# Two halves of the activations through one high weight matrix in the down projections

## The reference

```python
# first_block, twice: w_down is 4096 x 1024
hn = rmsnorm(h, gains[2])
ff = jnp.square(jax.nn.relu(hn @ w_up[layer])) @ w_down[layer]
h = h + rmsnorm(ff, gains[3])
gate = jax.nn.sigmoid(h @ w_ple_gate[layer])
h = h + gate * (p[layer] @ w_ple[layer])
# second_block, twice: ffn_w_down is 2816 x 1024
gate = _causal_dwconv(xn @ ffn_w_gate[l], ffn_conv_w[l], ffn_conv_b[l])
x = x + (jax.nn.silu(gate) * (xn @ ffn_w_up[l])) @ ffn_w_down[l]
```

## Time and profile before

| | |
|---|---|
| three runs | 1644.57, 1646.49, 1647.23 us |
| the profiled execution | 1639.38 us |
| its span, first to last instruction | 1637.9 us |
| TensorE matmuls: busy, count | 1492.3 us, 10862 |
| VectorE: busy, count | 1024.2 us, 1491 |
| ScalarE: busy, count | 778.5 us, 1205 |
| mean granted TensorE clock | 0.955 |
| DMA | 228.44 MB, mean 139 GB/s |

### The profile page before, as it was taken

One profiled execution on the slowest core, in us unless ns is written; L12 is line 12 of the kernel. 1 busy time (PEld: TensorE's weight loads), 2 busy tenths in 40 slices (PEclk: granted clock), 3 DMA queues, 4 the chain that ended last, 5 costly groups with the idle time before them and its releaser, 6 DMA issues.

```text
span 1637.9 us, 26038 instructions
## 1 busy us (share of the span) xinstructions
PE 1492.3 (91%) x10862; PEld 1406.7 (86%) x10862; DVE 1024.2 (63%) x1491; ACT 778.5 (48%) x1205; POOL 158.1 (10%) x136
## 2 busy tenths in 40 slices
PE   6877987999998877999999998899999988999999
PEld 5865877999987667999998787799999777899999
DVE  4653447765467855665467675577866666587763
ACT  5322424544446453444336666444445666554443
POOL 0002232110000001211010000011000000011100
PEclk9988998999999999999999997999999998899999
DMA  7431203555545314465544421355556431246563
GB/s 240 129 103 52 99 5 106 177 182 180 182 154 179 128 53 129 135 194 185 186 154 155 143 87 52 97 172 168 188 180 198 142 113 52 78 145 189 167 199 101
DMA packets 186388, 228.44 MB, mean 139 GB/s; under 512 B 5920, under 2 KB 161056, under 8 KB 186272
## 3 DMA queue, kind: packets, MB, share of 16 engines
q1 hardware_dynamic: 185264, 222.01, 42.2%
q0 software_dynamic: 1008, 4.77, 0.8%
HBM read 225.72 MB, written 1.05 MB: 138 GB/s over the span
## 4 chain that ended last, share of the span: by engine, by line
PE 65%; DVE 20%; ACT 9%; issue 4%; POOL 0%; DMA 0%; ACTq 0%; DVEq 0%; SPq 0%; POOLq 0%
PE bank L492 19%; PE bank L493 18%; PE bank L494 18%; DVE weights_low L767 7%; ACT weights_high L665 5%; PE bank L500 2%; PE bank L1894 2%; PE bank L974 2%; DVE cv L2732 2%; ACT S L1944 2%; PE bank L1873 1%; DVE cv L2729 1%; DVE S L2018 1%; DVE pad L2719 1%; DVE h L868 1%
## 5 line engine op out<-in xcount | busy, mean ns | idle before, releaser
L767 DVE TENSOR_TENSOR weights_low<-weights_raw,weights_high 128x1024 fp32r<-128x1024 f32 (+3 forms) x421 | 507.2, 1224 | 380.2 <-ACT weights_high L665 379.7
L665 ACT CAST weights_high<-weights_raw 128x1024 fp32r<-128x1024 f32 (+3 forms) x421 | 424.4, 1030 | 330.5 <-PE bank L494 330.3
L492 PE MATMUL bank<-hT_high,weights_high 128*128 128x256 f32 (+1 forms) x1672 | 487.5, 292 | 49.1 <-DVE hT_low L850 21.6
L493 PE MATMUL bank<-hT_low,weights_high 128*128 128x256 f32 (+1 forms) x1672 | 482.5, 289 | 0.0
L494 PE MATMUL bank<-hT_high,weights_low 128*128 128x256 f32 (+1 forms) x1672 | 482.0, 288 | 0.0
L492 PEld LDWEIGHTS bank<-hT_high,weights_high 128*128 128x128 f32 (+1 forms) x1672 | 330.0, 197 | 56.8 <-issue 28.6
L493 PEld LDWEIGHTS bank<-hT_low,weights_high 128*128 128x128 f32 (+1 forms) x1672 | 329.9, 197 | 0.5
L494 PEld LDWEIGHTS bank<-hT_high,weights_low 128*128 128x128 f32 (+1 forms) x1672 | 329.4, 197 | 0.5
L492 PE MATMUL bank<-aT_high,weights_high 128*128 128x256 f32 x864 | 242.2, 280 | 0.2
L493 PE MATMUL bank<-aT_low,weights_high 128*128 128x256 f32 x864 | 241.3, 279 | 0.0
L494 PE MATMUL bank<-aT_high,weights_low 128*128 128x256 f32 x864 | 241.1, 279 | 0.0
(11 more groups left out here) (409 smaller groups left out, 1877.1 us busy)
## 6 DMA issues: line engine op xcount, KB each, us to landing
weights_raw<-in_w_up SPq DMA_DIRECT2D x32, 1024.0 KB, 5.3
weights_raw<-in_w_down SPq DMA_DIRECT2D x32, 1024.0 KB, 5.1
weights_raw<-in_ffn_w_gate SPq DMA_DIRECT2D x22, 1024.0 KB, 5.3
weights_raw<-in_ffn_w_up SPq DMA_DIRECT2D x22, 1024.0 KB, 5.3
weights_raw<-in_w_in SPq DMA_DIRECT2D x20, 1024.0 KB, 5.1
weights_raw<-in_w_in_ab SPq DMA_DIRECT2D x16, 1024.0 KB, 5.8
weights_raw<-in_ffn_w_down SPq DMA_DIRECT2D x16, 1024.0 KB, 5.2
weights_raw<-in_w_o SPq DMA_DIRECT2D x10, 1024.0 KB, 4.9
```

The lines of the kernel that those rows point to most:

```text
L492: k.E.matmul(out, xh, wh, start=first, stop=False)
L493: k.E.matmul(out, xh, wl, start=False, stop=False)
L665: k.A.copy(w.halves(n)[0], w.raw_part(n)).then_inc(*k.s.weight_high(n))
L767: k.V.tensor_tensor(low, w.raw_part(n), high.bitcast(F32), ALU.subtract).then_inc(*k.s.weight_low(n))
```

## The change

In the four down projections (both ff1, both ff2) the high and the low half of `aT` now lie in one tensor with a leading dimension of two. One matmul with the high weights streams both halves, 2 x 256 columns, into a whole bank: columns 0 to 255 get high weights times high activations, columns 256 to 511 high weights times low activations. One matmul with the low weights streams the high half and adds to columns 0 to 255. The two halves of the bank are added when it is read. A pair p now takes two banks, one for each output tile, with a signal each. In ff1 ScalarE first copies the second half of each bank to `u`, VectorE adds the first half to it, ScalarE squares `u`, and VectorE multiplies it by the gain. In ff2 VectorE adds the second halves, then the first halves, to `h`. All other products are left as they were.

```diff
     def pair(name, *shape, side="left"):
-        return cut(name + "_high", *shape, dt=F32R, side=side), cut(name + "_low", *shape, dt=F32R, side=side)
+        both = cut(name, 2, *shape, dt=F32R, side=side)
+        return [both[:, i] for i in range(2)], both
...
-        m.hT, m.aT, m.u = k.hT, pair("aT", DFF1 // P, SEQ), shaped(both, DC, SEQ)
+        m.hT, (m.aT, m.aT_both), m.u = k.hT, pair("aT", DFF1 // P, SEQ), shaped(both, DC, SEQ)
...
+def tensor_whole_panels(k, st, p, both, chunks, key, ready):
+    banks = [k.banks.fill((st, "out", p, b)) for b in range(2)]
+    for k0 in range(0, chunks, 8):
+        n, nk = k.w.first_part[k.w.take(key + (k0, 256 * p))], min(8, chunks - k0) // 2
+        for i in range(2):
+            k.E.wait_ge(*k.s.weight_low.at(n + i))
+            high, low = k.w.halves(n + i)
+            last = k0 + 8 >= chunks and i == 1
+            for b in range(2):
+                for d in range(nk):
+                    c, at = k0 + i * nk + d, slice(b * P, (b + 1) * P)
+                    if p == 0 and b == 0:
+                        k.E.wait_ge(*ready(c))
+                    k.E.matmul(banks[b][:, :], high[:, d, at], both[:, :, c, :], start=(c == 0), stop=False)
+                    mm = k.E.matmul(banks[b][:, 0:SEQ], low[:, d, at], both[:, 0, c, :], start=False, stop=(c == chunks - 1))
+                keys = ([("half", n + i)] if b else []) + ([(st, "out", p, b)] if last else [])
+                if keys:
+                    mm.then_inc(*k.s.products(*keys))
...
 def residual_after(k, st, p):
-    return k.banks.was_read((st, "out", p)) if st[0] in ("m2", "ff2") else k.s.residual.at((st, p))
+    if st[0] == "ff2":
+        return k.banks.was_read((st, "out", p, 1))
+    return k.banks.was_read((st, "out", p)) if st[0] == "m2" else k.s.residual.at((st, p))
...
+def vector_whole(k, st, p, u):
+    for b in range(2):
+        key = (st, "out", p, b)
+        k.V.wait_ge(*k.s.low_copied.at(key))
+        k.V.tensor_tensor(u[:, 2 * p + b, :], u[:, 2 * p + b, :], k.banks[key][:, 0:SEQ], ALU.add).then_inc(*k.banks.read(key))
+
+def vector_add_whole(k, st, p):
+    for half_at in (slice(SEQ, 512), slice(0, SEQ)):
+        for b in range(2):
+            key, h = (st, "out", p, b), k.h[:, 2 * p + b, :]
+            if half_at.start:
+                k.V.wait_ge(*k.s.products.at(key))
+                k.V.tensor_tensor(h, h, k.banks[key][:, half_at], ALU.add).then_inc(*k.s.half_added((st, p, b)))
+            else:
+                k.V.wait_ge(*k.s.half_added.at((st, p, b)))
+                k.V.tensor_tensor(h, h, k.banks[key][:, half_at], ALU.add).then_inc(*k.banks.read(key))
...
@@ scalar_feed_forward_1
             scalar_split(k, k.w.first(("down", layer, k0, 256 * p)) + 2)
-        scalar_out_squares(k, st, p)
+        for b in range(2):
+            key = (st, "out", p, b)
+            A.wait_ge(*s.products.at(key))
+            A.copy(m.u[:, 2 * p + b, :], k.banks[key][:, SEQ:512]).then_inc(*s.low_copied(key))
+        for b in range(2):
+            A.wait_ge(*k.banks.was_read((st, "out", p, b)))
+        scalar_pair_square(k, (st, "post"), p, m.u[:, 2 * p:2 * p + 2, :].rearrange("p k n -> p (k n)"))
...
@@ vector_feed_forward_1
             vector_split(k, k.w.first(("down", layer, k0, 256 * p)) + 2)
-        vector_out_gained(k, st, p, m.u, post_gain(k, layer, 1))
+        vector_whole(k, st, p, m.u)
+        u, gain = m.u[:, 2 * p:2 * p + 2, :], post_gain(k, layer, 1)[:, 2 * p:2 * p + 2]
+        V.wait_ge(*s.pair_squares.at(((st, "post"), p)))
+        V.tensor_tensor(u, u, spread(gain, 2, SEQ), ALU.mult).then_inc(*s.step())
...
@@ vector_feed_forward_2
-        vector_add_out(k, st, p)
+        vector_add_whole(k, st, p)
```

More of the change, by code:

```diff
@@ L157 @@
 BY_SCALAR = ["weight_high", "residual_high", "pair_squares", "turned_high", "squares", "root", "silu", "logs", "decayed", "relu_high", "gated_high",
-             "exps", "sink_exps", "trig", "lam_exps", "feature_squares"]
+             "exps", "sink_exps", "trig", "lam_exps", "feature_squares", "low_copied"]
 BY_VECTOR = ["weight_low", "residual_low", "factored", "mean", "inverse", "diagonal", "residual", "step", "gates", "conv", "spread_gates", "inverse_n",
-             "head_mean", "mixed", "angles", "active", "forget", "row_max", "sink_max", "reduced", "normed", "turned",
+             "head_mean", "mixed", "angles", "active", "half_added", "forget", "row_max", "sink_max", "reduced", "normed", "turned",
              "lam", "gated_up", "exp_sums", "minus_sink"]
@@ L422, in allocate @@
             m = k.mem = Memory()
-            m.memT, m.inv = [pair("memT", DC, SEQ, side="right") for _ in range(2)], right("mem_inv", NT)
+            m.memT, m.inv = [pair("memT", DC, SEQ, side="right")[0] for _ in range(2)], right("mem_inv", NT)
             scope()
@@ L438, in allocate @@
         m.r, m.sq = [shaped(both[:, i * 1024:(i + 1) * 1024], 2, 512) for i in range(2)]
-        m.hT, m.aT, m.u = k.hT, pair("aT", DFF1 // P, SEQ), shaped(both, DC, SEQ)
-        m.R, m.Rp, m.pt, m.pT = cut("factor", SEQ), cut("post_factor", SEQ), cut("pt", NT, 256), pair("pT", 2, SEQ)
+        m.hT, (m.aT, m.aT_both), m.u = k.hT, pair("aT", DFF1 // P, SEQ), shaped(both, DC, SEQ)
+        m.R, m.Rp, m.pt, m.pT = cut("factor", SEQ), cut("post_factor", SEQ), cut("pt", NT, 256), pair("pT", 2, SEQ)[0]
         if layer == 0:
@@ L447, in allocate @@
         m = k.ple[layer] = Memory()
-        m.hT, m.gate, m.emb = pair("gate_hT", DC, SEQ), cut("gate", 4, 512), cut("emb", 4, 512)
+        m.hT, m.gate, m.emb = pair("gate_hT", DC, SEQ)[0], cut("gate", 4, 512), cut("emb", 4, 512)
         close()
@@ L472, in allocate @@
         m = k.ff2[l] = Memory()
-        m.hT, m.aT, m.pad, m.cv = k.hT, pair("aT", DFF2 // P, SEQ), cut("pad", 2, 2, SEQ + 2), cut("cv", 3, 2, SEQ)
+        m.hT, (m.aT, m.aT_both), m.pad, m.cv = k.hT, pair("aT", DFF2 // P, SEQ), cut("pad", 2, 2, SEQ + 2), cut("cv", 3, 2, SEQ)
         m.R, m.out = cut("factor", SEQ), cut("out", NT, D)
@@ L1553, in tensor_feed_forward_1 @@
     for p in range(4):
-        tensor_pair_panels(k, st, p, m.aT, DFF1 // P, ("down", layer), lambda c: s.active.at((st, c - c % 2)))
+        tensor_whole_panels(k, st, p, m.aT_both, DFF1 // P, ("down", layer), lambda c: s.active.at((st, c - c % 2)))
     tensor_sums(k, (st, "post"))
@@ L2656, in tensor_feed_forward_2 @@
     for p in range(4):
-        tensor_pair_panels(k, st, p, m.aT, DFF2 // P, ("down_2", l), lambda c: k.s.active.at((st, c - c % 2)))
+        tensor_whole_panels(k, st, p, m.aT_both, DFF2 // P, ("down_2", l), lambda c: k.s.active.at((st, c - c % 2)))
         if l == 1 and p:
```

## The result

The changed kernel takes 1648.5 us (median of 20 runs, 1641.55 to 1652.34) where the kernel before, in 20 runs beside it, takes 1644.7 (1639.22 to 1647.23). The ratio is 1.0028 [1.0019, 1.0038], that is 4.6 us slower (3.1 to 6.2). Forecast were 4.4 us faster.

What follows compares the result with a forecast made beforehand. The prediction took TensorE alone to bound the down projections. Streams -9.6, ends of ff1 +4.1, ends of ff2 +0.7 and +0.4, clock 0, sum -4.4 us: 1646.5 to 1642.1 us, range 1638.8 to 1649.2.

Steps and rivals of the forecast that it cites:

- The streams: Down projections: 864 triples of narrow matmuls become one wide and one narrow each, saving 11.1 ns apiece, 9.6 us.
- The fixed part: Part of a matmul's time that doesn't grow with its columns: 13.3 ns over hT, 11.1 ns over aT.
- The bound that I had taken from memT's slowest row: Slowest 512-column row at full clock, 234.0 ns per wide matmul, leaving a gain of 1.4 us in the streams.
- rival C: Break between halves, or addresses, slows the wide stream to 234.0 ns: 3.8 us slower, 1650.3 us; chance 0.11.
- Rival E: Fixed part grows with columns, wide matmul 235.6 ns: streams gain nothing, 5.2 us lost, 1651.7 us; chance 0.04.
- the prediction's own sum: Streams -9.6, ends of ff1 +4.1, ends of ff2 +0.7 and +0.4 (ends together +5.2): -4.4 us.
- The ends of ff1: After ff1's last matmul, copies and additions behind the weight split delay the squaring 2.07 us; two layers, 4.1 us lost.
- The ends of ff2: VectorE adds four times 256 instead of once 512: 0.7 us lost in layer 0, 0.4 in layer 1.
- The clock: Longer standstill before the sums may add or remove a 1.2 GHz stretch; counted 0, bounds 1.7 us either way per layer.
- Rival D's stretch: Clock falls in front of the sums in both layers: -2.1 us in all, 1644.4 us; chance 0.08.
- the stretch of the earlier trace: Half clock from 481.4 on, 3.4 us long; might go, gaining 1.7 us per layer, counted as 0.
- both rivals on that side: The slower side: rival C at 1650.3 us, chance 0.11, and Rival E at 1651.7 us, chance 0.04.

Runs made afterwards that it cites:

- x3: Changed kernel with the low weights streaming both halves too, so all matmuls are 512 columns wide; 1745.97 us (one run).
- x5: The work of x3 done in four matmuls of 256 columns per chunk and tile; 1753.66 us (one run).
- x7: x4 with the four wide matmuls of a tile and half first, then its four narrow ones; 1640.8 us, ratio 0.9978 to the kernel before.
- x9: x4 with all eight wide matmuls of a weight half first, then its eight narrow ones; 1636.02 us, ratio 0.995 to the kernel before.
- x17: x9 again with no edit, on the same chip as x16; 1637.23 us, ratio 0.9961 to the kernel before.
- x16: x9 with each wide matmul made two narrow ones, order and ends kept; 1643.6 us, ratio 0.9993 to the kernel before.
- x10: The changed kernel again with no edit, on the same chip as x11; 1648.45 us, ratio 1.0028 to the kernel before.
- x1: Changed kernel with both halves of each aT chunk side by side, so the wide matmul streams one block of 512; 1646.97 us, ratio 1.002.
- x6: Changed kernel without the product with the low weights, only wide matmuls left; 1550.84 us (one run).
- x2: Changed kernel with each wide matmul split into two of 256 columns, banks, copies and additions kept; 1644.84 us, ratio 1.0004 to the kernel before.
- x14: A single profile of x2 with no edit; 1647.98 us.
- x15: Another single profile of x2 with no edit; 1643.87 us.
- x11: x2 again with no edit, on the same chip as x10; 1645.59 us, ratio 1.0007 to the kernel before.
- x4: Changed kernel with the banks read ahead of the last weight split of a pair, in ff1 and ff2; 1644.43 us, ratio 0.9999 to the kernel before.
- x8: The kernel before with only the reads moved ahead of the last weight split; 1641.72 us, ratio 0.999.

## Why the prediction was wrong

**1. The streams: the step that failed.** It read: "If it stays with these operands, the 512-column matmul takes 213.3 + 11.1 = 224.4, the pair 342.2, and 864 x 11.1 = 9.6 us go". Measured: wide 233.7, narrow 120, pair 353.2, so 864 x 0.1, nothing. Two things were wrong in it.
- The fixed part was read from two streams over hT that differ in more than width: at 256 columns hT streams past the weights, at 512 the weights stream past hT. I took the difference for the price of 256 columns. Two widths with the same operands would have been needed, and the trace of before has no such pair. With everything else equal (x3 against x5) a merge is worth 6.9 ns in one stage and 2.6 in another, not 11.1.
- I priced each matmul as if it had one pace whatever stood around it. Wide and narrow in turn, what a merge brings is lost again: the wide one takes 233.7 ns and the narrow one 120. Regrouping gives it back (x7, x9, x17), and the order of the operands alone doesn't (x16). How much of this is the change of width itself isn't shown, because each width also has two paces in rows of its own: 117.8 and 113.3 ns, 233.3 and 228.9 (third and first stage of x3). Even the two slower ones make a pair of only 351.1, so at least 2.2 of the 353.3 ns are the change of width. The rest can be paces: the wide one's own slower pace costs 4.4, and in the third stage of x10 the pair in turn takes 348.9. What chooses the pace, no run shows.

The bound that I had taken from memT's slowest row, 234.0, was all but the value, and the row was nearer than I thought: I set it aside because hT had shown the same fixed part twice. Above 229.6 ns the kernel is slower, said rival C, and that held, though its reason (the break) is refuted by x1. Rival E had the right gain, nil. Its size for the wide matmul, 235.6, is refuted (x6), but not its idea that nothing is fixed: the mean of the two wide paces, 231.1, is just the sum of the two narrow ones. Corrected by the measured pair, the prediction's own sum is -0.1 + 5.2 = +5.1 against 4.6 (3.1 to 6.2) measured. That it fits so well is in part luck, as part 4 says.

The Trainium skill's rule (TensorE: Matmul & The Clock Gate, Back-to-back issue gap), N / 2.4 + 2.5 ns, gives 109.2 and 215.8 ns as estimates for the two widths. The traces disagree: at full clock the quickest rows of equal matmuls take 113.3 and 226.7 ns. Its small fixed part was nonetheless nearer to the outcome than my 11.1.

**2. The ends of ff1: right at the ends themselves.** Predicted 2.07 us later, measured 2.10 at the square, 2.13 at the reciprocal, with the subtraction between, as described. For p 0 to 2 nothing shows: the stages didn't grow.

**3. The ends of ff2: right.** At the very end, timeline of the chain:

```profile
1641.77 0.14 PE bank L651
...
1641.93 0.42 DVE h L921
1642.35 0.67 DVE h L924 x2
```

Three additions, 1.10 us, for 0.70: 0.4 as predicted. In layer 0 the additions end and the reciprocal starts later by 0.7, as the chain shows, first before, then after:

```profile
1259.57 0.13 PE bank L494
...
1268.38 1.77 DVE factor L821
```

```profile
1265.34 0.13 PE bank L651
...
1267.87 0.66 DVE h L921 x2
1268.53 0.67 DVE h L924 x2
...
1274.88 1.76 DVE factor L846
```

9.54 us for 8.81: 0.73.

**4. The clock: not nothing, and it blurs the total.** Rival D's stretch came: in the changed kernel the granted clock was 0.50 here, in the embedding, where before it fell later, in the gate's product.

```profile
477.00:480.40 3.40, 3.40 (x18) 3.40 (x17) 3.06 (x3) 0.24 (x1) 1.29 (x1) 0.50 0.46 158
```

It lay on work with slack: the gate's product still waits 0.58 us for `gate_hT` afterwards, where it waited 2.33. And the stretch of the earlier trace rows is gone, which the prediction had named and put at 0. The gate's product from its first matmul's start to its last one's, before and after:

```profile
479.72:504.26 24.54, 24.35 (x192) 24.15 (x193) 20.02 (x25) 16.67 (x23) 1.41 (x1) 0.93 0.47 149
```

```profile
484.50:507.51 23.01, 22.84 (x191) 22.64 (x192) 19.92 (x25) 16.69 (x23) 1.41 (x1) 1.00 0.48 157
```

It is 1.5 us shorter, and 1.4 in layer 1 (24.44 and 23.01). So the gate's last matmul starts 36.01 us after the last one of the down projection, for 35.40 before: 0.6 us later, not 2.1. The same 23.0 stands in both layers of x1, x2, x10, x14 and x15, which all have the longer ends, and in one layer of x11. In x4 and x16, with the reads moved ahead, it is 24.5 again, and 24.1 to 24.5 in the three profiles of the kernel before (x8 has 23.0 and 24.3). **This is the second step that failed:** the clock was counted as 0, though with bounds of 1.7 in each layer, and here it paid back 2.6 to 3.0 us. With it the corrected sum is +2.1 to +2.5, and 0.6 to 4.1 us of the measured loss lie where the prediction priced nothing. x4 shows the same from the other side: of the 4.7 us at its ends the gate's product takes back 3.1, and still the ratios have it 4.8 faster (2.4 to 7.2). On which rows the rest lies isn't shown.

Stretches at 1.2 GHz also lie elsewhere from one execution to the next of the same kernel, and single times differ by up to 8 us (1639.38 against 1647.12). The narrow kernels x2 and x11 have all of the ends' 5.3 us in their chain (2 x 2.1, 0.7 and 0.4) and show 0.7 to 1.2 us of them in the total. The gate's product pays part of that back. The mean granted clock over the runs goes the same way: 0.9536 in x2 and 0.9529 in x11, for 0.9516 and 0.9503 in the kernel before beside them, while x10 has 0.9510. Between x10 and x11 that is 0.0019 of 1645 us, by my estimate 3.1 us of full clock, the size of the 3 us by which they differ. **It stays open** what grants the one more than the other. Two smaller things are part of it. Some 0.3 us of the mean lie outside the span: three of x10's ten executions have 1.8 to 3.1 us there, all of x11's 1.4 to 1.5. And in single executions one stage is at a quicker pace: narrow matmuls in x11's profile (61.76 for 63.3 us), x15's (60.29 for 62.4) and x8's (62.13), wide ones in x10's (61.71 for 62.4, with 230.6 ns for 234.3).

The predicted range held the median, 1648.5, by luck. In differences it went from -7.7 to +2.7, and 4.6 lies outside; the kernel before took 1644.7 in these runs, 1.8 less than the 1646.5 on which the forecast stood. The chance of 0.15 for slower was too small, since both rivals on that side hung on one derived number.

## What to carry to other kernels

A fixed cost per instruction may be read from two sizes only if nothing but the size differs between them, the operand that streams included, and only after the same instruction has been looked at in several stages: here its pace varied by 4.4 ns, which is the size of what was to be gained. When matmuls are merged, keep equal widths next to each other: here wide ones in rows of eight saved 7 us in the four stages, and wide ones alternating with narrow ones nothing at all. And when an engine's queue holds a long job for a buffer released by the last matmul, read the results first: that alone took the changed kernel from 1.0028 to 0.9999. A delay on the chain need not reach the total: follow it to the end of the next product and look at the granted clock there.

## What the runs showed of the hardware that was not expected

- **The neighbours of a matmul count.** Pairs of 512 and 256 columns take 353.3 ns in turn and 344.5 in rows of eight (x9), while three of 256 take 353.4 in either order (x16). At least 2.2 of the 8.8 ns are the change of width; the rest can be the paces of the last point.
- **A moving operand in two blocks** costs no more than one in a single block (x1: stages equal within 0.03 us).
- **Both widths have two paces at full clock,** 113.3 and 117.8 ns for 256 columns, 228.9 and 233.3 for 512 over `aT`, in the same code from one stage or execution to the next. In the 12 profiles of kernels whose down projections have matmuls of one width only, the pace never changed within an unbroken row, only where TensorE had waited or done other matmuls in between (x3's fourth stage above, and x5, x6, x8, x11, x15). The embedding's matmuls over `pT` in layer 0 show both: first before, then after, past the stretch at half clock.

```profile
474.85 0.28 PE L492 MATMUL bank<-pT_high,weights_high 128*128 128x256 f32 x1
...
476.89 0.28 PE L492 MATMUL bank<-pT_high,weights_high 128*128 128x256 f32 x1
```

```profile
480.58 0.28 PE L493 MATMUL bank<-pT,weights_high 128*128 128x256 f32 x1
...
481.40 0.28 PE L494 MATMUL bank<-pT,weights_high 128*128 128x256 f32 x1
```

18 distances of 113.3 ns in the one, seven of 117 in the other. In layer 1 it was the other way round. What chooses the pace, no run shows.
